# Six copies of x into the row table, issued behind the last strip of the first attention stage

## The reference

```
for layer in range(2):
    h = rms_norm(x, g_mix[layer])
    a, b, c = dilated_attention(h), mla_attention(h), neighbourhood_attention(h)     # 6 + 6 + 4 heads
    x = x + concat(rms_norm(a), rms_norm(b), rms_norm(c)) @ w_o[layer]
    h = rms_norm(x, g_ffn[layer])
    if layer == 0: x = x + (silu(h @ w1) * (h @ w3)) @ w2                            # 1024 -> 2816 -> 1024
    else:          x = x + moe_swiglu(h, w_router, e_w1, e_w3, e_w2)                 # top 2 of 8, 1024 -> 3584 -> 1024
return rms_norm(x, g_final)
```

## Time and profile before

| | us |
|---|---|
| median of 3 runs (2481.55 to 2484.16) | 2483.45 |
| the profiled execution | 2487.08 |
| its span, first to last instruction | 2485.4 |
| PE busy in the span (96%) | 2393.0 |
| DVE busy (30%) | 739.6 |
| ACT busy (23%) | 571.5 |
| POOL busy (5%) | 121.1 |
| mean granted clock of TensorE, as a share of full speed | 0.984 |

### The profile page before, as it was taken

One profiled execution on the slowest core, in us unless ns is written; L12 is line 12 of the kernel. 1 busy time (PEld: TensorE's weight loads), 2 busy tenths in 40 slices (PEclk: granted clock), 3 DMA queues, 4 the chain that ended last, 5 costly groups with the idle time before them and its releaser, 6 DMA issues.

```text
span 2485.4 us, 40198 instructions
## 1 busy us (share of the span) xinstructions
PE 2393.0 (96%) x16824; PEld 2236.3 (90%) x16825; DVE 739.6 (30%) x1499; ACT 571.5 (23%) x1116; POOL 121.1 (5%) x108
## 2 busy tenths in 40 slices
PE   7999998999999999989989999999989999999998
PEld 7988876788879888779989989999989999999996
DVE  5566742434745566640000000010000010100104
ACT  3355521222433454421010001010010010100102
POOL 1130100000001120010000000000000000000001
PEclk9999999999999999999999999999999999999999
DMA  8210247323220210467766666778867687787883
GB/s 259 94 50 1 83 125 256 119 75 126 110 104 28 85 50 8 150 257 285 288 227 247 234 229 221 293 258 300 302 238 284 238 325 294 284 299 289 326 304 121
DMA packets 204711, 488.68 MB, mean 197 GB/s; under 512 B 5105, under 2 KB 31872, under 8 KB 204144
## 3 DMA queue, kind: packets, MB, share of 16 engines
q1 hardware_dynamic: 193408, 434.60, 47.7%
q0 software_dynamic: 8944, 42.91, 5.5%
q10 hardware_dynamic: 2176, 8.39, 0.8%
HBM read 465.17 MB, written 37.49 MB: 202 GB/s over the span
## 4 chain that ended last, share of the span: by engine, by line
PE 89%; DVE 4%; DMA 3%; issue 2%; ACT 2%; SPq 0%; DVEq 0%; ACTq 0%
PE ps L1084 35%; PE ps L1099 17%; PE ps L983 9%; PE ps L788 5%; PE ps L994 5%; PE ps L934 4%; PE ps L766 3%; DMA weight_ring<-in_w_dram 2%; PE ps L808 1%; PE ps L809 1%; PE ps L811 1%; PE ps L799 1%; PE ps L800 1%; PE ps L801 1%; PE ps L1040 1%
## 5 line engine op out<-in xcount | busy, mean ns | idle before, releaser
L1084 PE MATMUL ps<-hT,attention_arena 128*128 128x132 f32 (+3 forms) x4096 | 528.6, 285 | 22.7 <-issue 21.8
L1084 PEld LDWEIGHTS ps<-hT,attention_arena 128*128 128x128 f32 x4096 | 509.7, 191 | 24.5 <-issue 24.5
L1894 DVE TENSOR_TENSOR attention_arena<-ps,attention_arena 128x256 f32<-128x256 f32 x224 | 95.1, 425 | 1202.9 <-ACT attention_arena L1428 1202.9
L1084 PE MATMUL ps<-hT,weight_ring 128*128 128x132 f32 (+3 forms) x3072 | 395.4, 284 | 0.0
L1084 PEld LDWEIGHTS ps<-hT,weight_ring 128*128 128x128 f32 x3072 | 380.6, 190 | 0.0
L1428 ACT ACTIVATE attention_arena<-ps 128x256 f32<-128x256 f32 x224 | 85.8, 383 | 1131.9 <-PE ps L1084 1131.8
L1099 PE MATMUL ps<-attention_arena 128*128 128x132 f32 (+3 forms) x2048 | 266.7, 283 | 0.0
L1099 PEld LDWEIGHTS ps<-attention_arena 128*128 128x128 f32 x2048 | 254.6, 190 | 0.0
L983 PE MATMUL ps<-x_high,w_parts 128*128 128x512 f32 x704 | 225.8, 402 | 11.6 <-DVE w_parts L1642 10.0
L1099 PE MATMUL ps<-attention_arena,weight_ring 128*128 128x132 f32 (+3 forms) x1536 | 200.0, 283 | 0.0
L1099 PEld LDWEIGHTS ps<-attention_arena,weight_ring 128*128 128x128 f32 x1536 | 190.9, 190 | 0.0
(11 more groups left out here) (268 smaller groups left out, 2615.1 us busy)
## 6 DMA issues: line engine op xcount, KB each, us to landing
attention_arena<-in_e_w_dram SPq DMA_DIRECT2D x96, 2048.0 KB, 12.3
weight_ring<-in_e_w_dram SPq DMA_DIRECT2D x72, 2048.0 KB, 12.2
weight_ring<-in_w_dram SPq DMA_DIRECT2D x22, 1024.0 KB, 7.8
weight_ring<-in_w_dram SPq DMA_DIRECT2D x4, 2816.0 KB, 11.0
weight_ring<-in_w_o_dram SPq DMA_DIRECT2D x4, 2048.0 KB, 7.9
attention_arena<-rows_by_slot POOLq DMA_DIRECT2D x8, 1024.0 KB, 11.6
results_by_slot<-attention_arena ACTq DMA_DIRECT2D x8, 1024.0 KB, 10.2
weight_ring<-in_w_in_dram SPq DMA_DIRECT2D x2, 3072.0 KB, 11.2
```

Of the source, the lines that this page charges most:

```text
L1084: last = nc.tensor.matmul(ps[:, f % 2, m * UNIT:m * UNIT + n], w[:, k, i * P:(i + 1) * P], XT[:, k, 0:n], start=(k == 0), stop=(k == ND - 1))
L1894: tt(eh[:, f % EHS, :], ps[:, f % 2, UNIT:2 * UNIT], esil[:, f % 2, :], ALU.mult).then_inc(gu_free, 1)
```

## The change

The loop that issues the six copies moves up, from behind the gains and the wait for the third gate product to right behind the last strip of layer 0. The wait for the gate product is dropped. Nothing else is changed.

```
                if l == 0:
-
+                    for i in range((NU + 1) * UNIT // SEQ):
+                        pool.dma_start(rows_dram[UNIT + i * SEQ:UNIT + (i + 1) * SEQ, :], a["x"][0]).then_inc(filled_before, 16)
                     pool.wait_ge(gains_free, 1)
                     for dst, src in layer_gains(1):
                         pool.dma_start(dst, src.partition_broadcast(P)).then_inc(gains_in, 16)
-                    pool.wait_ge(filled, J.filled(0, "g", 2))
-                    for i in range((NU + 1) * UNIT // SEQ):
-                        pool.dma_start(rows_dram[UNIT + i * SEQ:UNIT + (i + 1) * SEQ, :], a["x"][0]).then_inc(filled_before, 16)
```

## The result

| | us |
|---|---|
| before, median of 4 runs (2481.55 to 2484.23) | 2483.80 |
| changed, median of 4 runs (2497.80 to 2503.75) | 2500.48 |
| ratio changed / before, with its 95% interval | 1.0062 (1.0048 to 1.0075) |
| profiled execution of the changed kernel, its span | 2503.75, 2502.1 |
| forecast (range) | 2496 (2491 to 2506) |

The kernel became slower by 16.7 us in this comparison. A second one, with five runs of the changed kernel beside fifteen of before, gave +12.3 us (2498.31 against 2486.05, ratio 1.0049, 1.0035 to 1.0063). The forecast was +12.7.

What follows compares the result with a forecast made beforehand. PE, busy 96% of the span, was taken as the bound, losing time only where it waits. Loss 25.1 us less gain 12.4 us gave +12.7 us on the runs' median 2483.45: forecast 2496, 8-in-10 range 2491 to 2506.

Steps and rivals of the forecast that it cites:

- The stall of the dense stage goes: Dense stage: the starved weight load lands in time, removing PE's 10.2 us stall and 2.2 us slow restart; gain 12.4 us.
- w_o is starved, and PE with it: Output projection: copies delay w_o's second half, so PE's first product of the second tile starts 22.9 us later (22.1 to 25.9).
- the landing: Second half of w_o lands at 325.7, between 324.9 and 326.6; upper bound 328.7; copies' last landing at 322.9.
- The way from ACT's piece to PE's product: From ACT's first piece of w_o's second half to DVE finishing the second tile's low part, releasing PE: 3.66 us.
- The slow restart: After waiting for w_o, PE restarts at the lower clock level: 2.2 us lost, bound 2.8.
- The reload of x and the first chunk are covered: Behind w_o: x's reload lands from 327.0 to 330.9, covered; the first w1 and w3 chunk keeps its 7.84 us.
- The sum: Loss 25.1 us less gain 12.4 us: +12.7 us, bounds +11.9 and +16.3.
- the engines share by bytes: Rival: w_o gets half the engines or slips through, lands about 295, nothing replaces the stall; -12.4 us, 2471; chance 0.10.
- the copies take 10 us more here: Rival, part of the longer wait: copies at the new place last 10 us more; 2506 to 2508; chance 0.05 for both parts.
- POOL issues late: Rival: copies start 8 us or more behind SP's loads, so the first chunk lands at 338.7; 2479; chance 0.04.
- the dense stall has another cause: Rival, part of the longer wait: the dense-stage stall stays; 2506 to 2508; chance 0.05 for both parts.

Runs made afterwards that it cites:

- quiet_place: Changed kernel with the six copies issued two strips earlier, behind the eighth strip of the first attention stage instead of the tenth; 2476.08 us, 0.9955 of before.
- reload_behind_w_o: Changed kernel, but SP issues the reload of x only when the second half of w_o has landed; 2500.93 us, 1.0054 of before.
- changed_again: The changed kernel's text unaltered, run once more for its scatter; 2498.31 us, 1.0049 of before.
- cut_new_place: Changed kernel with each copy split in two by columns, contiguous pieces of 2 KB instead of 64 KB, same bytes and place; 2479.73 us, 0.9967 of before.
- cut_old_place: Kernel before, copies left in the dense stage but each split in two by columns into 2 KB pieces; 2475.29 us, 0.9954 of before.

## Why the prediction was right

**The stall of the dense stage goes (12.4 us).** Right. In the first profile after, the stretch from the start of the dense stage to the products with `w2` is 632.90 - 385.29 = 247.6 us; before it was 617.21 - 356.66 = 260.55: 12.9 less. quiet_place has it alone: 248.17 us, 12.4 less. In the second profile of the changed kernel the stretch is 248.24 us, 12.3 less.

**w_o is starved, and PE with it (22.9 us).** Right in place, chain and releaser. PE's first product of the second tile moved from 306.46 to 333.12, and in the second profile to 330.85: 26.7 and 24.4. Of the first, 1.0 us does not come from the copies: the whole stage ran that much later before they were issued, POOL's last strip from 280.23 against 279.13 and SP's issue of `w_o` at 284.29 against 283.29. Without it 25.7 is still inside the bounds that I gave, 22.1 to 25.9, but near the upper end, not the value that I took.

The term that was mis-sized is the landing. From POOL's first issue to the landing of `w_o` it was to be 325.7 - 282.0 = 43.7 us; it was 330.1 - 282.9 = 47.2 and 327.85 - 281.7 = 46.2. Two parts of it were too small. I had the copies last 40.9 us, as in the dense stage; from the first issue to the last landing they took 285.4 + 40.7 - 282.9 = 43.2 us and 284.2 + 39.0 - 281.7 = 41.5. And I had `w_o` land 2.8 us behind them, the middle of the range in which the engines come free; it landed 4.0 and 4.7 us behind them. For the second part my reading is that a load has landed when the last of its engines is done, so that the latest engine sets the time and not the middle one: in 324 to 326 SP's queue is not yet at full rate (295 packets in 2 us against 395 alone). That reading agrees with reload_behind_w_o, which leaves no other load to blame, but it is not shown: no view here tells which engine was late. Why the copies take longer here stays open.

The way from ACT's piece to PE's product came out 0.7 us shorter than taken: 333.12 - 330.14 = 3.0, not 3.66.

**The slow restart (2.2 us, bound 2.8).** Right in kind. The first 13 products, from 333.12 to 338.81, take 5.69 us instead of 13 x 0.232 = 3.0, 2.7 us; the granted clock is 0.50 in 333.0 to 338.8 and 1.00 in 339 to 341. In changed_again it is 9 products up to 334.72, 3.87 us instead of 2.1, 1.8 us, at a granted clock of 0.52 in 331.0 to 334.7.

**The reload of x and the first chunk are covered.** Right, the first with less room than forecast. I had SP issue the reload by 285.9, as before, and its first quarter land at 327.0; SP's issues took until 325.75 (see below), and the first quarter landed 46.7 us after its issue, at 331.4. DVE's first addition, at 334.11, still shows no wait. The chunk lands in 7.78 us.

**The sum.** Up to the products with `w2` it is 632.90 - 617.21 = +15.7 in the first profile and 631.30 - 617.21 = +14.1 in the second, against a forecast of +12.7 and bounds of +11.9 and +16.3. The +16.7 of the first comparison lies just above these bounds, and that the second comparison came within half a us of +12.7 is partly luck: its profile has PE's wait 1.5 us longer than forecast as well.

**The rest of the 16.7 us** is most likely not from the change. In the first profile the loop over the experts starts 14.3 us later than before (1122.59 against 1108.31), and the span ends 16.7 later. From +15.7 to +14.3 is within what that part of the kernel varies: from the first product with `w2` to the loop it takes 489.6 to 491.1 us in the nine profiles. The step from 14.3 to 16.7 comes at the restarts behind the branch to the next unit. The first 64 products of the second, third and fifth unit, in the chain of waits before:

```profile
1270.90 11.30 PE ps L1084 x64
...
1482.69 9.51 PE ps L1084 x64
...
1814.66 10.96 PE ps L1084 x64
```

and in the changed kernel:

```profile
1285.43 12.58 PE ps L1082 x64
...
1498.49 10.16 PE ps L1082 x64
...
1831.16 11.28 PE ps L1082 x64
```

The same products take 1.28, 0.65 and 0.32 us longer, 2.25 in all. No step of the change reaches that stage, and it is the one profile of before that stands apart: at the first of these places all eight profiles of edited kernels have 12.23 to 12.73 (quiet_place, which is faster, 12.33), at the second 9.99 to 10.16. That also fits quiet_place's span, which ends 11.0 us before that of before though its products with `w2` start 12.65 earlier. Whether this one profile is an outlier, or any edit brings the longer restarts, is not shown. The second profile of the changed kernel ends 14.3 us later than before.

**The rivals.** That the engines share by bytes is out: with the same bytes in smaller pieces, in cut_new_place, the landing of `w_o` falls by half. That whole transfers are served in order of issue is out by cut_old_place, and by the changed kernel itself: of its six copies, issued from 282.9 to 285.4 by POOL's rows, three come after the issue of `w_o` at 284.29, and it landed behind all six. That the copies take 10 us more here is out: 2.3 and 0.6. That POOL issues late is out by its row, 282.90. That the dense stall has another cause is out by quiet_place and cut_old_place.

## What to carry to other kernels

A bulk copy with no deadline is not free in the background: while it ran here, a load with small packets got about one packet for each of the copy's (239 against 255), so its place must be free of loads that something waits for, from the first issue to the last landing. Look for such a place in the DMA rows of the trace and compare its length with the copy's (here 41 us of copies in some 67 us of idle engines, from 190 to 257: -10.3 us). Where there is none, cut the copy's contiguous pieces: with the same bytes, at the old place, PE's wait fell from 10 us to 1.

## What was not expected of the hardware

While the copies held the engines, SP itself stood still. The four issues of the reload, which took 2.21 us before, took 41 us, in SP's timeline of the changed kernel:

```profile
284.70 41.05 SPq L598 DMA_DIRECT2D x_rows<-in_x_dram  x4
```

Nothing was queued behind them on SP that was due, so it cost nothing here. A deadline load that SP had to issue behind them would have been late; no run here has one.

The copies of contiguous rows went in large packets (11.47 MB in 255, 45 KB on average), and the copies in 2 KB pieces did not go in 2 KB packets (12.58 MB in 3264, 3.9 KB on average). The latter agrees with the Trainium skill (DMA: Bandwidth & Descriptors, section on SWDGE, HWDGE and iDMA), which calls packets of up to 4096 B the preferred size; the former exceeds it by a factor of eleven, and here the measurement decides.

The stretch of products at a granted clock of about 0.5, after a wait of about 25 us, was 5.7 us in one profile and 3.9 in another of the same program.
